# Chunked scan: the decays' exponent is bounded by a minimum on VectorE, the causal mask moves to the scores, and the product with the scores runs one group later

## Chip, cores and metric

One of the eight cores of a Trainium2 chip runs the whole kernel in one launch. The metric is the device time of that core in microseconds, the median of several runs. The other cores are idle.

## Reference, cut to what matters

The reference computes two transformer-like layers over 512 tokens of width 1024. The change touches one part of the first layer, the state-space scan with 16 heads and 2 groups:

```python
a_cs = jnp.cumsum(a_dt, axis=-1)                                   # a_dt = dt * a, never positive
seg = a_cs[..., :, None] - a_cs[..., None, :]
decay = jnp.exp(jnp.where(causal, seg, -jnp.inf))
scores = jnp.einsum('bclgn,bcsgn->bgcls', cc, bc)
attn = scores[:, :, None] * decay
y_diag = jnp.einsum('bgrcls,bcsgrp->bclgrp', attn, x_dt)
```

For each head, the scores of its group are multiplied by exp(sum at l minus sum at s) where s is not after l, and by zero elsewhere. The sums never grow along the sequence, so the exponent is at most zero wherever the mask lets it through. The kernel uses chunks of 128 tokens, which gives the same y.

## The kernel before

**Work and staging.** TensorE runs one long stream of matmuls. Large products with weights (`gemm`, blocks of 512 columns) are cut into eight slices each. A float32 product is made of three matmuls of rounded parts (high by high, high by low, low by high), so a slice of a feature block holds six matmuls of 512 columns. The smaller steps of the layer (scan, attention, norms) are woven in between the slices. All engines walk through one list of steps, written by a planner (`plan`, line 82, the weave of the scan at line 176), and each engine issues its part of every step in the order of that list and waits on semaphores. An engine's queue is strictly in order, so a wait holds back all that comes behind it on that engine.

**Weights.** SyncE loads a block of weights in two pieces into `wraw` (line 797). ScalarE rounds a piece into `whi` (`round_weights`, line 1278) and VectorE takes the rest, `wlo = wraw - whi` (`rest_of_weights`, line 1632). For block m they are issued at slices 0 and 2 (rounding) and 2 and 4 (rest) of the block before (line 246). SyncE waits for `wlo` before it loads that `wraw` again.

**The scan.** There are four chunks c of 128 tokens and for each of them five steps `("ssd", c, part)`. Steps 0 to 3 each handle a group of four heads, step 4 finishes the chunk. Three slices of the k and q products lie between two steps (four after one of the chunks). The intermediate tiles are one large tensor in SBUF, which the profile calls `arena` (`sc`, `ee`, `xdt`, `xs` and others); PSUM tiles are `bank`. In a step with part below 4:

- TensorE (line 1155): at part 0 two score matmuls. Then the exponents of the group, into one bank of 128 by 512: an identity times a mask tile (0 or -1e30, bfloat16, line 1167), and on top of it a matrix of ones times `b_hi` (line 1170), which gives the running sum at l for four heads. Then, from part 1 on, `y_diag(part - 1)`: four matmuls with `ee` as the stationary operand (line 1146), eight instructions of 64 columns in the profile.
- ScalarE (line 1591): four exponentials from the bank into `ee`, with the negated sum at s as the bias, 128 columns each.
- VectorE: at part 0 a copy of the scores to SBUF (line 2043). Then `ee` times the scores (line 2048), which `y_diag` waits for.
- GpSimd: spreads the sums of a later group into `b_hi` (`decays`, line 2201, operation at line 2207), up to four groups ahead, and at part 0 makes `xdt`, `xdd` and the skip term (lines 2229, 2233, 2236), 1024 columns each.

Two banks are used in turn for scores, exponents and chunk states (`plan_aux`, `free_aux` at line 861), and each next user waits for the reader of the one before.

**Where the weights' rests lie between the steps of the scan.** In the order of VectorE, between `("ssd", c, 0)` and `("ssd", c, 1)` stands one rest in chunks 0, 1 and 2, and two stand there in chunk 3. Between parts 1 and 2 there is none in any chunk. Between parts 2 and 3 there are two in chunk 0 and one in each of the others. Between parts 3 and 4 there is none in chunk 0 and one in the others. In the order of ScalarE the rounding of the piece for the second of two such rests comes behind the exponentials of the step ahead of it, and so does that for the one rest between parts 2 and 3 of chunk 3.

Of the kernel before, what the change touches and what calls it, by code (L numbers as in the profile page):

```python
# [23 lines left out]
ALU = mybir.AluOpType  # L24
ACT = mybir.ActivationFunctionType
# [6 lines left out]
P = 128  # L32
# [342 lines left out]
def plan_aux():  # L375

    ring = Ring(2)
    for s in STEPS:
        if s[0] == "xturn":
            ring.use(s, "S")  # L380
        if s[0] == "ssd_decay":
            ring.use("decay", "V")
        if s[0] == "ssd":
            _, c, part = s
            if part == 0:
                ring.use(("scores", c), "V")
            if part < 4:
                ring.use(("decay", c, part), "S")
            if part == 4:
                for g in range(2):  # L390
                    if c > 0:
                        ring.use(("y_off", c, g), "V")
                for g in range(2):
                    if c < NT - 1:
                        ring.use(("state", c, g), "V")
    return ring


AUX = plan_aux()
# [106 lines left out]
def emit(nc, dram, spill, out):  # L506
    ctx = ExitStack()
    with ctx:
# [3 lines left out]
        def sem(name):  # L512
            return ctx.enter_context(nc.semaphore(name))
# [9 lines left out]
        b_hi, b_lo = sb("b_hi", [P, NK, T], F32R), sb("b_lo", [P, NK, T], F32R)  # L523
# [27 lines left out]
        bank = [ctx.enter_context(nc.psum_tensor(f"bank{i}", [P, 512], F32)) for i in range(8)]  # L551

        ident = cst[:, CST.at("ident")]
        tri = cst[:, CST.at("tri")]
# [6 lines left out]
        identb = cstb[:, CSTB.at("ident")]  # L561
        strict = cstb[:, CSTB.at("strict")]
        after = cstb[:, CSTB.at("after")]
# [13 lines left out]
        sc = mem(60, [2, P])  # L577
        ee = mem(61, [2, 4, P])
# [85 lines left out]
        acs_n = small(64)  # L664
# [19 lines left out]
        s_sw = sem("s_small_weights")  # L684
        s_cst, s_ident = sem("s_constants"), sem("s_identity")
        s_tri, s_hg = sem("s_decays_spread"), sem("s_hgrn_gated")
        s_x = [sem(f"s_x{t}") for t in range(NT)]
        s_row = {name: sem("s_row_" + name) for name in ROWS}
        s_yz, s_spill, s_back = sem("s_gated"), sem("s_residual_stored"), sem("s_residual_back")
# [160 lines left out]
        def _(pe):  # L850
            def mm(o, lhsT, rhs, start, stop, **kw):
                return nc.tensor.matmul(o, lhsT, rhs, start=start, stop=stop, **kw)  # L852
# [290 lines left out]
            def ssd(c, part):  # L1143
                ts = slice(P * c, P * c + P)

                def y_diag(j):
                    pe.wait_ge(s_attn, 4 * c + j + 1)
                    if j == 0:
                        pe.wait_ge(s_xd, 2 * c + 1)
                        if c >= 1:  # L1150
                            pe.wait_ge(s_y, c)
                    for i in range(4):
                        h = 4 * j + i
                        last = mm(bank[6 + j // 2][:, (h % 8) * HD:(h % 8) * HD + HD], ee[:, j % 2, i, :],
                                  xdt[:, c % 2, h * HD:h * HD + HD], True, True)
                    last.then_inc(s_yd, 1)

                if part == 0:
                    pe.wait_ge(s_cx, XC)
                    ps = free_aux(("scores", c))  # L1160
                    for g in range(2):
                        last = mm(ps[:, P * g:P * g + P], bct[:, g, ts], bct[:, 2 + g, ts], True, True)
                    last.then_inc(s_aux, 1)
                if part < 4:
                    pe.wait_ge(s_cst, 32)
                    ps = free_aux(("decay", c, part))
                    mm(ps[:, :], identb, after.unsqueeze(1).to_broadcast([P, 4, P]), True, False)
                    n = 4 * c + part
                    pe.wait_ge(s_tri, n + 1)
                    mm(ps[:, :], ones_r, b_hi[:, n % 4, :], False, True).then_inc(s_aux, 1)  # L1170
                    if part >= 1:
                        y_diag(part - 1)
                if part == 4:
                    if c > 0:
                        pe.wait_ge(s_st, 2 * c)
                        for g in range(2):
                            ps = free_aux(("y_off", c, g))
                            mm(ps[:, :], bct[:, 2 + g, ts], state[:, g, :], True, True).then_inc(s_aux, 1)
                    y_diag(3)
                    if c < NT - 1:  # L1180
                        pe.wait_ge(s_xd, 2 * c + 2)
                        for g in range(2):
                            ps = free_aux(("state", c, g))
                            mm(ps[:, :], btok[:, c, P * g:P * g + P], xdd[:, 512 * g:512 * g + 512], True, True)\
                                .then_inc(s_aux, 1)
# [75 lines left out]
        def _(act):  # L1261
# [254 lines left out]
            for s in STEPS:  # L1516
# [64 lines left out]
                    A(dtend, t64[2], ACT.Exp).then_inc(s_ex, 1)  # L1581
                if s[0] == "ssd" and s[2] < 4:
                    _, c, j = s
                    key = ("decay", c, j)
                    act.wait_ge(s_aux, AUX.at[key] + 1)
                    n_ = 4 * c + j
                    if n_ >= 2:
                        act.wait_ge(s_yd, n_ - 1)
                    for i in range(4):
                        col = SH * c + 4 * j + i  # L1590
                        last = A(ee[:, j % 2, i, :], bank[4 + AUX.slot(key)][:, P * i:P * i + P], ACT.Exp,
                                 bias=acs_n[:, col:col + 1])
                    last.then_inc(s_auxend["S"], 1)
                if s[0] == "stack":
                    act.wait_ge(*end_sem("q"))
                    for i in range(3):
# [13 lines left out]
        def _(dve):  # L1610
# [4 lines left out]
            def link(ins):  # L1615

                chain[0] += 1
                ins.then_inc(s_vc, 1)
                dve.wait_ge(s_vc, chain[0])
# [419 lines left out]
            def ssd(c, part):  # L2039
                if part == 0:  # L2040
                    key = ("scores", c)
                    dve.wait_ge(s_aux, AUX.at[key] + 1)
                    link(v.tensor_copy(sc, bank[4 + AUX.slot(key)][:, 0:2 * P].rearrange("p (a b) -> p a b", b=P)))
                    dve.sem_inc(s_auxend["V"], 1)
                if part < 4:
                    dve.wait_ge(s_auxend["S"], AUX.ends[AUX.at[("decay", c, part)]][1])
                    e = ee[:, part % 2, :, :]
                    v.tensor_tensor(e, e, sc[:, part // 2, :].unsqueeze(1).to_broadcast([P, 4, P]), ALU.mult).then_inc(s_attn, 1)
                if part == 4:
                    bc = lambda t, g: t[:, SH * c + 8 * g:SH * c + 8 * g + 8].unsqueeze(2).to_broadcast([P, 8, HD])  # L2050
                    if c > 0:
                        for g in range(2):
                            key = ("y_off", c, g)
                            dve.wait_ge(s_aux, AUX.at[key] + 1)
                            link(v.tensor_tensor(h64(ytmp[:, g, :]), h64(bank[4 + AUX.slot(key)][:, :]), bc(ecs, g), ALU.mult))
                            dve.sem_inc(s_auxend["V"], 1)
                    dve.wait_ge(s_yd, 4 * c + 4)
                    dve.wait_ge(s_xd, 2 * c + 2)
                    for g in range(2):
                        y, x = ytmp[:, g, :], xs[:, c, 512 * g:512 * g + 512]  # L2060
                        if c > 0:
                            link(v.tensor_tensor(y, y, bank[6 + g][:, :], ALU.add))
                            ins = v.tensor_tensor(x, x, y, ALU.add)
                        else:
                            ins = v.tensor_tensor(x, bank[6 + g][:, :], x, ALU.add)
                    ins.then_inc(s_y, 1)
                    if c < NT - 1:
                        for g in range(2):
                            key = ("state", c, g)
                            if c > 0:  # L2070
                                link(v.tensor_tensor(h64(state[:, g, :]), h64(state[:, g, :]), bc(edec, g), ALU.mult))
                            dve.wait_ge(s_aux, AUX.at[key] + 1)
                            ps = bank[4 + AUX.slot(key)][:, :]
                            if c > 0:
                                ins = v.tensor_tensor(state[:, g, :], state[:, g, :], ps, ALU.add)
                            else:
                                ins = v.tensor_copy(state[:, g, :], ps)
                            ins.then_inc(s_st, 1)
                            dve.wait_ge(s_st, 2 * c + g + 1)
                            dve.sem_inc(s_auxend["V"], 1)  # L2080
# [253 lines left out]
```

## Time and profile before

| | before |
|---|---|
| median of 3 runs | 1382.84 us (1381.85 to 1383.66) |
| the profiled execution's own time | 1382.09 us |
| span in the profile | 1380.3 us |
| TensorE matmul busy | 1358.2 us (98%) |
| VectorE busy | 756.0 us (55%) |
| ScalarE busy | 609.0 us (44%) |
| GpSimd busy | 57.0 us (4%) |
| the scan's steps | from 97.94 us to about 213 us of the span |

The profiled execution is 0.75 us under the median, and 1.8 us of it lie outside the span. Engines overlap, so busy times do not add up. Starts and durations of matmuls are modelled, and a matmul is shown as longer than the distance to the next one, because they are pipelined: what counts is the distance between starts. "Idle before" at the end of a row names what the engine waited for. The granted clock of TensorE is 1.0 of full speed (2.4 GHz) in all 40 slices of the page.

### The profile page before, as it was taken

To read this page: it belongs to the slowest core of one execution; us is meant where nothing else is said; L and a number is where in the kernel's file an instruction comes from. 1 tells how busy PE (TensorE), PEld (TensorE's weight loads), DVE (VectorE), ACT (ScalarE), POOL (GpSimd) and SP (SyncE) were. 2 spreads that over 40 slices of the span, in tenths; PEclk is the share of its full clock that TensorE was granted. 3 is DMA by queue.
4 is the path that set the end of the run, shared out by engine and by line. 5 is a ranking of instruction groups with operands and counts; after the bars stand their busy time and mean duration, and the time that the engine had idled before them with its cause. 6 is when DMAs were issued, how large, how long until landed. Compare 5 with 4: busy or idle time off the path is not lost. (4 is left out here: it accounts for less than half of the span.)

```text
span 1380.3 us, 17992 instructions
## 1 busy us (share of the span) xinstructions
PE 1358.2 (98%) x7051; PEld 1127.5 (82%) x7055; DVE 756.0 (55%) x1180; ACT 609.0 (44%) x1129; POOL 57.0 (4%) x38
## 2 busy tenths in 40 slices
PE   9999999999999999999999999999999999999999
PEld 7888778888888888887778777888898888888887
DVE  5775554457656563435457776767555334443333
ACT  6554332457777533224426567773243222221221
POOL 0025310000000000000010000000000000000000
PEclk9999999999999999999999999999999999999999
DMA  4222223252111344232441100102313332232323
GB/s 167 91 77 76 63 76 99 84 145 69 47 47 62 110 150 147 92 101 71 149 133 62 61 17 16 32 1 107 123 62 107 96 103 92 92 106 93 101 82 107
DMA packets 35349, 121.27 MB, mean 88 GB/s; under 512 B 3908, under 2 KB 5188, under 8 KB 35010
## 3 DMA queue, kind: packets, MB, share of 16 engines
q1 hardware_dynamic: 34690, 119.07, 26.6%
q10 hardware_dynamic: 576, 1.05, 0.4%
q8 instruction: 57, 0.93, 0.3%
q14 instruction: 26, 0.21, 0.1%
HBM read 112.77 MB, written 4.19 MB: 85 GB/s over the span
## 5 line engine op out<-in xcount | busy, mean ns | idle before, releaser
L852 PE MATMUL bank<-a_hi,whi 128*128 128x512 f32 (+1 forms) x880 | 345.9, 393 | 0.5 <-DVE a_lo L2132 0.5
L852 PE MATMUL bank<-a_hi,wlo 128*128 128x512 f32 (+1 forms) x880 | 336.7, 383 | 0.0
L852 PE MATMUL bank<-a_lo,whi 128*128 128x512 f32 (+1 forms) x880 | 336.1, 382 | 0.0
L1278 ACT ACTIVATE whi<-wraw 128x1024 fp32r<-128x1024 f32 x194 | 196.8, 1044 | 191.8 <-PE bank L852 162.2
L1632 DVE TENSOR_TENSOR wlo<-wraw,whi 128x1024 fp32r<-128x1024 f32 x194 | 241.2, 1253 | 66.5 <-ACT whi L1278 61.4
L852 PE MATMUL bank<-arena 128*128 128x128 f32 (+5 forms) x1332 | 184.3, 284 | 8.1 <-DVE arena L1994 2.6
L852 PEld LDWEIGHTS bank<-a_hi,wlo 128*128 128x128 f32 x880 | 165.4, 188 | 32.5
L852 PEld LDWEIGHTS bank<-a_hi,whi 128*128 128x128 f32 x880 | 165.8, 188 | 31.7 <-issue 2.4
L852 PEld LDWEIGHTS bank<-a_lo,whi 128*128 128x128 f32 x880 | 165.8, 188 | 30.8 <-issue 1.4
L852 PEld LDWEIGHTS bank<-arena 128*128 128x128 f32 (+1 forms) x1332 | 164.7, 189 | 18.0 <-issue 6.4
L852 PE MATMUL bank<-whi,a_hi 128*128 128x512 f32 x288 | 114.7, 398 | 1.6 <-DVE wlo L1632 0.8
L852 PE MATMUL bank<-whi,a_lo 128*128 128x512 f32 x288 | 112.4, 390 | 0.0
L852 PE MATMUL bank<-wlo,a_hi 128*128 128x512 f32 x288 | 112.2, 389 | 0.0
L852 PE MATMUL bank<-whi,b_hi 128*128 128x512 f32 x240 | 93.8, 391 | 0.0
L852 PE MATMUL bank<-whi,b_lo 128*128 128x512 f32 x240 | 93.4, 389 | 0.0
L852 PE MATMUL bank<-wlo,b_hi 128*128 128x512 f32 x240 | 93.4, 389 | 0.0
L2113 DVE TENSOR_TENSOR_SCAN arena<-arena 128x128 f32<-128x128 f32 (+1 forms) x64 | 52.7, 823 | 58.4 <-ACT arena L1414 58.2
L1327 ACT ACTIVATE b_hi<-arena 128x512 fp32r<-128x512 f32 x30 | 19.0, 634 | 130.2 <-DVE arena L1742 118.3
L1296 ACT ACTIVATE arena<-bank 128x512 f32<-128x512 f32 x50 | 29.8, 597 | 80.8 <-PE bank L852 80.7
L852 PEld LDWEIGHTS bank<-whi,a_hi 128*128 128x128 f32 x288 | 54.1, 188 | 13.7 <-issue 1.8
L1732 DVE TENSOR_TENSOR arena<-arena,bank 128x512 f32<-128x512 f32 x32 | 22.0, 687 | 76.2 <-PE bank L852 76.0
L852 PEld LDWEIGHTS bank<-whi,a_lo 128*128 128x128 f32 x288 | 54.0, 188 | 11.6
(257 smaller groups left out, 1748.0 us busy)
## 6 DMA issues: line engine op xcount, KB each, us to landing
wraw<-in_wblk SPq DMA_DIRECT2D x190, 512.0 KB, 3.8
arena<-in_x SPq DMA_DIRECT2D x4, 512.0 KB, 6.1
arena<-in_x SPq DMA_DIRECT2D x1, 2048.0 KB, 7.9
spill<-arena SPq DMA_DIRECT2D x4, 512.0 KB, 7.8
arena<-spill SPq DMA_DIRECT2D x1, 2048.0 KB, 9.4
out<-arena SPq DMA_DIRECT2D x8, 256.0 KB, 2.5
arena<-arena SPq DMA_DIRECT2D x2, 896.0 KB
arena<-in_w1k SPq DMA_DIRECT2D x1, 1024.0 KB, 7.2
```

Source lines behind the costliest of these rows:

```text
L852: return nc.tensor.matmul(o, lhsT, rhs, start=start, stop=stop, **kw)
L1278: A(whi[n % 2][:, cols], wraw[i][:, 0:cols.stop - cols.start], ACT.Copy).then_inc(s_hi, 1)
L1296: ins = A(sgt[:, k % 2, :], bank[BANK[g]][:, :], ACT.Sigmoid, bias=bias)
L1327: A(b_hi[:, c, :], tt[:, p % 2, :], ACT.Copy).then_inc(s_tround, 1)
L1632: v.tensor_tensor(wlo[n % 2][:, cols], wraw[i][:, 0:cols.stop - cols.start], f32(whi[n % 2][:, cols]), ALU.subtract).then_inc(s_lo, 1)
L1732: v.tensor_tensor(x, x, ps[:, :], ALU.add).then_inc(s_end["V"], 1)
L2113: v.tensor_tensor_scan(w[:, ::-1], fail[:, ::-1], sig[:, ::-1], 0.0, ALU.mult, ALU.add)\
```

## The change

The mask product on TensorE is gone. Its place is taken by a minimum on VectorE, from the bank into `ee`, of the sum at l and the sum at the row's own s (`t64[0]`, which holds it for every row), so that the later exponential is at most one where the mask would be. The scores are multiplied by the causal matrix `tri` where they were copied. The exponentials work in place on `ee` in SBUF. The product with the scores for group part - 1 is issued on VectorE at the start of step part, ahead of the minimum of the group of that step, and for the last group at the start of step 4. The bank of the exponents is now released by VectorE. Two semaphores are new.

```diff
--- before.py
+++ after.py
@@ -385,7 +385,7 @@
             if part == 0:
                 ring.use(("scores", c), "V")
             if part < 4:
-                ring.use(("decay", c, part), "S")
+                ring.use(("decay", c, part), "V")
             if part == 4:
                 for g in range(2):
                     if c > 0:
@@ -684,6 +684,7 @@
         s_sw = sem("s_small_weights")
         s_cst, s_ident = sem("s_constants"), sem("s_identity")
         s_tri, s_hg = sem("s_decays_spread"), sem("s_hgrn_gated")
+        s_clamp, s_dexp = sem("s_exponents_clamped"), sem("s_decays_made")
         s_x = [sem(f"s_x{t}") for t in range(NT)]
         s_row = {name: sem("s_row_" + name) for name in ROWS}
         s_yz, s_spill, s_back = sem("s_gated"), sem("s_residual_stored"), sem("s_residual_back")
@@ -1162,12 +1163,10 @@
                         last = mm(ps[:, P * g:P * g + P], bct[:, g, ts], bct[:, 2 + g, ts], True, True)
                     last.then_inc(s_aux, 1)
                 if part < 4:
-                    pe.wait_ge(s_cst, 32)
                     ps = free_aux(("decay", c, part))
-                    mm(ps[:, :], identb, after.unsqueeze(1).to_broadcast([P, 4, P]), True, False)
                     n = 4 * c + part
                     pe.wait_ge(s_tri, n + 1)
-                    mm(ps[:, :], ones_r, b_hi[:, n % 4, :], False, True).then_inc(s_aux, 1)
+                    mm(ps[:, :], ones_r, b_hi[:, n % 4, :], True, True).then_inc(s_aux, 1)
                     if part >= 1:
                         y_diag(part - 1)
                 if part == 4:
@@ -1581,16 +1580,11 @@
                     A(dtend, t64[2], ACT.Exp).then_inc(s_ex, 1)
                 if s[0] == "ssd" and s[2] < 4:
                     _, c, j = s
-                    key = ("decay", c, j)
-                    act.wait_ge(s_aux, AUX.at[key] + 1)
-                    n_ = 4 * c + j
-                    if n_ >= 2:
-                        act.wait_ge(s_yd, n_ - 1)
+                    act.wait_ge(s_clamp, 4 * c + j + 1)
                     for i in range(4):
                         col = SH * c + 4 * j + i
-                        last = A(ee[:, j % 2, i, :], bank[4 + AUX.slot(key)][:, P * i:P * i + P], ACT.Exp,
-                                 bias=acs_n[:, col:col + 1])
-                    last.then_inc(s_auxend["S"], 1)
+                        last = A(ee[:, j % 2, i, :], ee[:, j % 2, i, :], ACT.Exp, bias=acs_n[:, col:col + 1])
+                    last.then_inc(s_dexp, 1)
                 if s[0] == "stack":
                     act.wait_ge(*end_sem("q"))
                     for i in range(3):
@@ -2040,12 +2034,23 @@
                 if part == 0:
                     key = ("scores", c)
                     dve.wait_ge(s_aux, AUX.at[key] + 1)
-                    link(v.tensor_copy(sc, bank[4 + AUX.slot(key)][:, 0:2 * P].rearrange("p (a b) -> p a b", b=P)))
+                    link(v.tensor_tensor(sc, bank[4 + AUX.slot(key)][:, 0:2 * P].rearrange("p (a b) -> p a b", b=P),
+                                         tri.unsqueeze(1).to_broadcast([P, 2, P]), ALU.mult))
                     dve.sem_inc(s_auxend["V"], 1)
+                if part >= 1:
+                    j = part - 1
+                    dve.wait_ge(s_dexp, 4 * c + part)
+                    e = ee[:, j % 2, :, :]
+                    v.tensor_tensor(e, e, sc[:, j // 2, :].unsqueeze(1).to_broadcast([P, 4, P]), ALU.mult).then_inc(s_attn, 1)
                 if part < 4:
-                    dve.wait_ge(s_auxend["S"], AUX.ends[AUX.at[("decay", c, part)]][1])
-                    e = ee[:, part % 2, :, :]
-                    v.tensor_tensor(e, e, sc[:, part // 2, :].unsqueeze(1).to_broadcast([P, 4, P]), ALU.mult).then_inc(s_attn, 1)
+                    key, n = ("decay", c, part), 4 * c + part
+                    dve.wait_ge(s_aux, AUX.at[key] + 1)
+                    if n >= 2:
+                        dve.wait_ge(s_yd, n - 1)
+                    link(v.tensor_tensor(ee[:, part % 2, :, :], bank[4 + AUX.slot(key)][:, :].rearrange("p (a b) -> p a b", b=P),
+                                         t64[0][:, 4 * n:4 * n + 4].unsqueeze(2).to_broadcast([P, 4, P]), ALU.min))
+                    dve.sem_inc(s_auxend["V"], 1)
+                    dve.sem_inc(s_clamp, 1)
                 if part == 4:
                     bc = lambda t, g: t[:, SH * c + 8 * g:SH * c + 8 * g + 8].unsqueeze(2).to_broadcast([P, 8, HD])
                     if c > 0:
```

## Rows read from the trace of the kernel before

**Rows 1.** Windows of the scan: sum and number of instructions of each engine, PE clock.

```profile
97.00:213.00 116.00, 116.00 (x561) 92.18 (x560) 62.98 (x65) 43.19 (x96) 43.59 (x25) 1.00 0.23 73
```

**Rows 2.** Timeline of TensorE around two groups of chunk 0: start us, duration us.

```profile
102.69 0.39 PE L852 MATMUL bank<-a_hi,wlo 128*128 128x512 f32 x1
...
102.92 0.39 PE L852 MATMUL bank<-cstb 128*128 128x512 bf16 x1
...
103.38 1.00 PE L852 MATMUL bank<-arena 128*128 128x64 f32 x8
...
108.40 0.39 PE L852 MATMUL bank<-cstb 128*128 128x512 bf16 x1
```

**Rows 3.** Groups of VectorE: the page, and by form from 98 to 212 us.

```profile
L1632 DVE TENSOR_TENSOR wlo<-wraw,whi 128x1024 fp32r<-128x1024 f32 x194 | 241.2, 1253 | 66.5 <-ACT whi L1278 61.4
...
L2055 DVE TENSOR_TENSOR arena<-bank,stat 128x512 f32<-128x512 f32 x6 | 4.2, 692 | 9.1 <-PE bank L852 9.1
```

**Rows 4.** Timeline of chunk 0's first group without TensorE; last, the skip term of chunk 3.

```profile
97.94 2.15 DVE L1632 TENSOR_TENSOR wlo<-wraw,whi 128x1024 fp32r<-128x1024 f32 x1 [1.23 <-ACT whi L1278]
...
98.95 2.89 POOL L2233 TENSOR_TENSOR arena<-arena,stat 128x1024 f32<-128x1024 f32 x1
...
99.35 1.28 ACT L1591 ACT_TABLE_LOAD   x1
...
100.00 0.41 DVE L2043 COPY arena<-bank 128x256 f32<-128x256 f32 x1
...
100.65 1.14 ACT L1591 ACTIVATE arena<-bank,stat 128x128 f32<-128x128 f32 x4
...
101.82 0.69 DVE L2048 TENSOR_TENSOR arena<-arena 128x512 f32<-128x512 f32 x1 [1.41 <-ACT arena L1591]
...
101.92 2.35 POOL L2236 TENSOR_TENSOR arena<-arena,vec 128x1024 f32<-128x1024 f32 x1
...
102.43 2.92 DVE L1632 TENSOR_TENSOR wlo<-wraw,whi 128x1024 fp32r<-128x1024 f32 x1
...
104.23 2.02 POOL L2207 TENSOR_TENSOR b_hi<-b_hi,cst 128x512 fp32r<-128x512 f32 x1
...
187.28 1.90 POOL L2236 TENSOR_TENSOR arena<-arena,vec 128x1024 f32<-128x1024 f32 x1 [18.69 <-DVE arena L2075]
```

**Rows 5.** Timeline of another stage: TensorE waits for VectorE and restarts.

```profile
942.45 0.68 DVE L1994 COPY arena<-bank 128x512 f32<-128x512 f32 x1
...
943.19 2.50 PE L852 MATMUL bank<-arena 128*128 128x128 f32 x20 [0.85 <-DVE arena L1994]
```

**Rows 6.** Timeline of chunk 1's first group.

```profile
125.19 2.76 POOL L2236 TENSOR_TENSOR arena<-arena,vec 128x1024 f32<-128x1024 f32 x1
...
126.75 0.43 DVE L2043 COPY arena<-bank 128x256 f32<-128x256 f32 x1 [0.56 <-PE bank L852]
...
127.91 1.04 POOL L2207 TENSOR_TENSOR b_hi<-b_hi,cst 128x512 fp32r<-128x512 f32 x1
...
131.55 1.00 PE L852 MATMUL bank<-arena 128*128 128x64 f32 x8
```

**Rows 7.** Timeline of chunk 2's first group.

```profile
158.05 2.77 POOL L2236 TENSOR_TENSOR arena<-arena,vec 128x1024 f32<-128x1024 f32 x1
...
158.97 0.41 DVE L2043 COPY arena<-bank 128x256 f32<-128x256 f32 x1
...
162.76 1.00 PE L852 MATMUL bank<-arena 128*128 128x64 f32 x8
```

**Rows 8.** Timeline of chunk 3's first group.

```profile
187.82 0.43 DVE L2043 COPY arena<-bank 128x256 f32<-128x256 f32 x1 [0.62 <-PE bank L852]
...
189.14 1.04 POOL L2207 TENSOR_TENSOR b_hi<-b_hi,cst 128x512 fp32r<-128x512 f32 x1
...
189.28 1.08 ACT L1278 ACTIVATE whi<-wraw 128x1024 fp32r<-128x1024 f32 x1
...
192.62 1.00 PE L852 MATMUL bank<-arena 128*128 128x64 f32 x8
```

## The prediction

> **What bounds the kernel now.** I read the page first, then the windows of the scan, then TensorE's timeline there, and last the timelines of the other engines around each product with the scores. The windows show TensorE busy for 116.00 us of 116.00, at full clock, with VectorE at 62.98 and ScalarE at 43.19 [rows 1]. So a matmul taken out of this stretch is worth its pitch at once, and any wait put on TensorE costs its length. TensorE's timeline gives the pitch as the distance between starts: 102.69 to 102.92 is 0.23 us for one matmul of 512 columns, and from the mask product at 102.92 to `y_diag` at 103.38 there are two such pitches, 0.46 us [rows 2]. The question is whether VectorE, which gets more to do and in another order, still delivers each `ee` before TensorE asks for it.
>
> **What it removes.** Sixteen mask products on TensorE at 0.23 us are 3.7 us, all on the path that sets the end. The wait for the constants that goes with them had long been met. Nothing is issued to a DMA queue by what moves, and SyncE's and GpSimd's own lists stay as they are.
>
> **What it adds.** Sixteen minimums from a bank with a broadcast operand from SBUF. The nearest row is of that very kind, bank and statistics to `arena`, 128 by 512: 692 ns [rows 3], in all 11 us on VectorE. The four score copies become products from the bank, at the same size, and I take the copy's 0.41 us [rows 4]. VectorE would be busy for 74 of the 116 us, so its load alone is covered. The exponentials stay at about 1.14 us for four [rows 4], now from SBUF; up to 0.2 us more would not change the sum, since below something else than they comes last in three chunks of four. Every bank is given back after the minimum, which is sooner than after the exponentials.
>
> **How VectorE and GpSimd share.** This sets the price of the new order. Alone, a `wlo` takes about 1.25 us on average [rows 3]. The one at 102.43 took 2.92 us and ended at 105.35, which is 1.08 after GpSimd's skip term ended at 104.27 (101.92 + 2.35). That skip term in turn took 2.35 where the same one of chunk 3, with no such product beside it, took 1.90, as it began to work only when VectorE's product ended at 102.51 [rows 4]. So in these rows each waits for the whole instruction of the other, then takes its turn, and VectorE's next one in line comes behind GpSimd's waiting one. The Trainium skill's page "SBUF — State Buffer", section "Who interferes with whom", says the same: a VectorE instruction with two SBUF inputs and a GpSimd one that reads SBUF lock each other out for whole instructions; the trace agrees with that. The score copy ran 0.41 us while GpSimd held the port [rows 4], so I take it that an instruction with a bank as source is not held.
>
> **The moved product.** The new order on VectorE is minimum, then the rests of weights that stand between the steps, then the product, then the next minimum. Before, the product came ahead of the rests. Where GpSimd is working, just after part 0 of each chunk, this is a row of turns. I work out when `y_diag(0)` can start, against when TensorE reaches it; the latter is 0.46 us earlier than now, as two mask products lie before it. A restart is put at 0.1 us after VectorE's end, since a wait elsewhere ended at 943.19 behind a copy that ended at 943.13 [rows 5].
> - Chunk 0. `wlo` ends at 100.09, scores at 100.41, minimum from 100.45 to 101.14. The next `wlo` waits for GpSimd's `xdd` to end at 101.84, and ends 1.08 later at 102.92. The skip term holds the port until 104.69 (1.77, as from 102.51 to 104.27). The product then takes 0.55 and ends at 105.24. The exponentials are done by 102.4 (by 103.7, if the table load of 1.28 us waited for them, which decides nothing). TensorE is there at 102.92, and restarts at 105.34: **2.4 us** lost [rows 4, 2].
> - Chunk 1. Scores end at 127.18, minimum at 127.94. GpSimd's spread begins at 127.91 and holds until 128.95; `wlo` to 130.03; the next spread about 1.0 to 131.0; product to 131.6. TensorE is there at 131.09: **0.6 us** [rows 6].
> - Chunk 2. Scores end at 159.38, minimum at 160.1. The skip term holds until 160.82; `wlo` to 161.9; a spread to 162.9; product to 163.4. TensorE is there at 162.30: **1.2 us** [rows 7].
> - Chunk 3. Scores end at 188.25, minimum at 189.0, exponentials at 190.2. The rounding behind them takes 1.08 to 191.3, which the second `wlo` needs. The first `wlo` runs from 189.18 to 190.3; two spreads in turn until 192.2, as the second `wlo` is not ready when the port comes free at 191.2; `wlo` to 193.3; product to 193.85. TensorE is there at 192.16: **1.8 us** [rows 4, 8].
>
> Between the later parts there is time enough. From one group's matmul to the next it was 5.48 us (102.92 to 108.40) [rows 2] and will be 5.25, and `y_diag` comes 0.23 behind: 5.5. The longest chain is chunk 0 from part 2 to 3 and the like in chunk 3: matmul 0.4, minimum 0.7, exponentials 1.15, rounding 1.08, `wlo` 1.25, product 0.6, together 5.2. It just fits, with 0.3 us to spare; I put 0 to 0.6 us on both together. All others lack the rounding, and fit with 2 us to spare even if GpSimd takes a turn.
>
> **Sum.** Less 3.7, plus 2.4 + 0.6 + 1.2 + 1.8 = 6.0: 2.3 us longer. Against the profiled execution's 1382.1 that is 1384.4; it stood 0.75 below the median, so against 1382.8 it is **1385.1 us**, 0.17% more. A measurement of this kernel can tell about 0.2% from no change, 2.8 us, so this is at the upper edge of "same". Nothing later gives the lost time back: it is matmuls that start later.
>
> **What isn't in the trace.** A minimum or product with one operand in a bank and one in SBUF while GpSimd works. From below it costs 0.69 or 0.41 us as taken above. From above it is held as the `ee` product was. The skill's page (same section) has the rule that one SBUF input at most does not contend; by it the sum stays as worked out, by the other it is that of the first rival. I take the lower end, because of the score copy, and keep the upper for the range.
>
> **Rivals.**
> - *The minimum and the masked scores are held by GpSimd too.* For: the second operand comes from SBUF, as that of the held ones did. Against: the copies ran free, but they have no second operand. Then, with the same turns, the product of chunk 0 ends at 106.8 instead of 105.2, chunk 1 at 132.2, chunk 2 (the skip term is under way when the scores come) at about 166.3, chunk 3 at about 195.1. The stalls are 4.0, 1.2, 4.1 and 3.0, together 12.3, less 3.7: 1391.4 us, slower. It turns slower as soon as the stalls pass 6.5 us. Slower by over 0.2% comes also from the forecast's own case if the small unknowns (restarts, semaphores that two more instructions pass on, the two tight chains) all cost: 0.6 us more is enough.
> - *The product is on time.* VectorE gets the port ahead of GpSimd when both wait, so that the rest and the product run back to back; then chunk 0 costs 0.7, chunk 3 about 0.9 for the rounding, the others nothing: 1382.8 − 3.7 + 1.6 = 1380.7. With no stall at all it is 1379.1. For: 1.4 to 2.4 us of idle time stand ahead of the products now. Against: the row at 102.43, in which the waiting GpSimd came first.
> - *TensorE's freed time is lost elsewhere, with no stall at `y_diag`:* the next waits would have to grow. TensorE had no wait in the stretch [rows 1], so I give this little.
>
> **How the numbers follow.** My case 0.65, spread from 1383.4 to 1388 (restart, tight chains, who is first in chunk 1). Held minimums 0.12, product on time 0.20, the last 0.03. Of my case about half lies above 1385.6. So slower by over 0.2%: 0.32 + 0.10 = 0.42. Faster by over 0.2% (under 1380.1): most of the product-on-time case with few stalls, 0.12. Same: 0.46. The range runs from 1379.5, which takes in nearly all of the on-time case, to 1389.5, which takes in my case's upper end and the weaker half of the held ones. The likeliest case's own range is 1383.4 to 1388.
>
> **What would show it.** Right: TensorE idle four times, just ahead of `y_diag(0)` of each chunk, released by the product on VectorE, longest in chunk 0; the period between groups at 5.25 us; a minimum of 0.69 us while GpSimd works; products of part 0 behind a `wlo`. Wrong: no idle time there and the scan 3.7 us shorter; a minimum of over 1 us; or idle time ahead of another part's `y_diag`, the two tight chains first.

## The result and the profile after

| | before | changed kernel |
|---|---|---|
| median | 1382.53 us (8 runs, 1381.59 to 1383.96) | 1386.79 us (8 runs, 1385.24 to 1389.31) |
| ratio to before | | 1.0031 [1.0022, 1.0040] |
| profiled execution, its span | 1382.09, 1380.3 us | 1385.24, 1383.4 us |
| VectorE busy | 756.0 us | 766.9 us |
| mean granted clock of the profiled execution | 1.000 | 0.997 |

The changed kernel is slower by 0.31%, 4.3 us. That is above the 0.2% line, and inside the range. The forecast was 1385.1, just under the line. The profiled execution is the fastest of the eight. Of all executions below one, in experiment 3, took 6525 us at a mean granted clock of 0.197; its profile is undisturbed up to 267 us, it counts in the median there (1384.32 us, 1384.2 without it) and not in the ratio.

TensorE had no wait in the scan before. In the changed kernel this is the whole list of its waits there (waiting line, what released it: us in total, times, longest):

```profile
PE bank L853 <- DVE arena L2044: 5.0, 4, 2.2
```

L2044 is the product of `ee` with the scores. TensorE's timeline of the changed kernel has the four waits, each ahead of the `y_diag(0)` of a chunk, with the idle time in brackets:

```profile
104.76 1.10 PE L853 MATMUL bank<-arena 128*128 128x64 f32 x8 [2.20 <-DVE arena L2044]
...
134.26 0.99 PE L853 MATMUL bank<-arena 128*128 128x64 f32 x7 [0.28 <-DVE arena L2044]
...
165.76 1.10 PE L853 MATMUL bank<-arena 128*128 128x64 f32 x8 [0.92 <-DVE arena L2044]
...
196.55 1.10 PE L853 MATMUL bank<-arena 128*128 128x64 f32 x8 [1.57 <-DVE arena L2044]
```

How the first of them comes about is in the timeline of the other engines in chunk 0 of the changed kernel, which answers to [rows 4]:

```profile
98.43 2.89 POOL L2238 TENSOR_TENSOR arena<-arena,stat 128x1024 f32<-128x1024 f32 x1
...
99.48 0.41 DVE L2037 TENSOR_TENSOR arena<-bank,cst 128x256 f32<-128x256 f32 x1
...
100.03 0.69 DVE L2050 TENSOR_TENSOR arena<-bank,stat 128x512 f32<-128x512 f32 x1
...
100.91 1.28 ACT L1586 ACTIVATE arena<-arena,stat 128x128 f32<-128x128 f32 x4 [0.80 <-DVEq L2053]
100.96 1.44 DVE L1626 TENSOR_TENSOR wlo<-wraw,whi 128x1024 fp32r<-128x1024 f32 x1 [0.24 <-DVE arena L2050]
...
101.40 2.76 POOL L2241 TENSOR_TENSOR arena<-arena,vec 128x1024 f32<-128x1024 f32 x1
...
102.17 0.39 PE L853 MATMUL bank<-b_hi 128*128 128x512 f32 x1
102.32 2.38 DVE L2044 TENSOR_TENSOR arena<-arena 128x512 f32<-128x512 f32 x1
104.12 4.93 POOL L2212 TENSOR_TENSOR b_hi<-b_hi,cst 128x512 fp32r<-128x512 f32 x4
```

The masked scores (L2037) and the minimum (L2050) take 0.41 and 0.69 us in the midst of GpSimd's `xdd` (98.43 to 101.32). The exponentials are done at 102.19. The rest of the weights ends at 102.40, and the product behind it takes 2.38 us, of which it works only the last 0.54: GpSimd's skip term has its turn until 104.16. TensorE, which issued its last matmul at 102.17, restarts at 104.76.

A second thing shows in the windows of the changed kernel (busy us with instructions of TensorE, weight loads, VectorE, ScalarE, GpSimd; then the granted clock):

```profile
106.00:108.00 2.00, 2.00 (x7) 1.56 (x6) 1.19 (x1) 0.78 (x3) 2.00 (x3) 0.59 0.00 0
108.00:110.00 2.00, 2.00 (x7) 1.59 (x6) 0.15 (x1) 1.55 (x2) 2.00 (x2) 0.56 0.00 0
110.00:196.00 86.00, 83.78 (x398) 66.43 (x396) 55.01 (x61) 30.77 (x66) 30.17 (x18) 1.00 0.20 64
196.00:200.00 4.00, 3.45 (x16) 2.99 (x17) 1.79 (x3) 1.28 (x4) 0.00 (x0) 0.81 0.65 207
200.00:215.00 15.00, 15.00 (x68) 11.94 (x68) 5.21 (x7) 5.66 (x12) 0.00 (x0) 0.94 0.20 72
```

TensorE's clock was 1.00 in the whole scan before [rows 1]. Now it falls from 2.4 GHz to the level of 1.2 GHz twice, shortly behind the waits of 2.20 and 1.57 us; behind those of 0.28 and 0.92 us it stays up. In the timeline the distance between starts goes from 0.23 to 0.43 us:

```profile
106.53 0.63 PE L853 MATMUL bank<-a_hi,whi 128*128 128x512 f32 x1
...
106.96 0.63 PE L853 MATMUL bank<-a_lo,whi 128*128 128x512 f32 x1
...
107.39 0.63 PE L853 MATMUL bank<-a_hi,wlo 128*128 128x512 f32 x1
```

The windows give the price of a fall: 2 × 0.41 + 2 × 0.44 = 1.7 us for the first, 4 × 0.19 + 15 × 0.06 = 1.7 us for the second.

**The sum, measured.** From the first score matmul to the start of the last addition of `y` the scan took 115.53 us before (97.94 to 213.47) and takes 121.32 us now (97.41 to 218.73), 5.8 more. From matmul to matmul, the waits cost 2.36, 0.44, 1.08 and 1.73 us, together 5.6. With −3.7 for the mask products and 3.4 for the clock that is 5.3. The 0.5 us left are found in two places. Behind a wait `y_diag` itself takes 0.91 us to the next matmul (104.76 to 105.67), and 0.81 where it doesn't wait (103.38 to 104.19 before), which is 0.1 in each of four chunks. And a mask product was worth 0.22 us rather than 0.23, 3.5 us in all (see below).

The profiled span grew by only 3.1 us, because this execution was 0.5 us ahead when the scan began, took 1.8 us less in a stage between about 650 and 710 us, and made up 0.4 us in smaller amounts behind it. In that stage ScalarE's roundings wait for weights to land, here the same one in the kernel before and in the changed kernel:

```profile
656.08 1.06 ACT L1278 ACTIVATE whi<-wraw 128x1024 fp32r<-128x1024 f32 x1 [3.24 <-DMA wraw<-in_wblk]
660.99 1.06 ACT L1277 ACTIVATE whi<-wraw 128x1024 fp32r<-128x1024 f32 x1 [2.90 <-DMA wraw<-in_wblk]
```

So what the stage takes differs with the landings. From a wait of TensorE at 651 us to one at 787 us (times of the kernel before) it is 135.9 us before, 134.1 in the changed kernel and 136.5 in another execution of the changed kernel (below), whose time is 1387.8. The saving isn't there each time, and a difference of 2 us between the spans of two profiles is no measure of a change to the scan.

### The profile page after: what moved, and what is told of

Same layout as the page of the kernel before. It is cut to its first block and busy times, and to the rows that moved or that the text cites. A ratio compares the mean times of both kernels' runs of the same rounds, so it can differ in the third digit from the quotient of the medians.

```text
span 1383.4 us, 18008 instructions
## 1 busy us (share of the span) xinstructions
PE 1358.5 (98%) x7035; PEld 1128.3 (82%) x7039; DVE 766.9 (55%) x1196; ACT 611.5 (44%) x1129; POOL 56.9 (4%) x38
## 2 busy tenths in 40 slices
DMA packets 35349, 121.27 MB, mean 88 GB/s; under 512 B 3908, under 2 KB 5188, under 8 KB 35010
```

## The experiments

Experiments 1 to 4 ran on one chip, where the kernel before had 1382.25 us (27 runs). The second profile of experiment 3 and experiment 5 are from another, where it had 1382.85 us (15 runs). A ratio with its interval is not the quotient of the two medians given, and can differ from it by 0.0008, about 1 us.

The scan, from the first score matmul to the start of the last addition of `y`, can be measured in each profile without the rest of the kernel. "Sum" is −3.5 us for the mask products where they are gone, plus the waits from matmul to matmul, 0.1 for each wait and 1.7 for each fall of the clock:

| profile | waits, us | falls in the scan | sum, us | scan against before's 115.53, us |
|---|---|---|---|---|
| changed kernel | 5.6 (4) | 2 | 5.9 | 5.8 |
| changed kernel, run again | 5.6 (4) | 2 | 5.9 | 5.7 |
| experiment 1 | 2.6 (2) | 0 | −0.7 | −0.6 |
| experiment 2 | 3.7 (3) | 0 | 4.0 | 4.0 |
| experiment 3, second profile | 4.6 (4) | 0 | 1.5 | 1.5 |
| experiment 4 | 2.0 (3) | 0 | −1.2 | −1.1 |
| experiment 5 | 5.6 (4), most of it filled | 0 | 2.5 | 2.6 |

These few terms account for the scan of every kernel within 0.2 us. The prices of the terms come from the same profiles, but one set of them fits all seven.

### 1. The product put back, ahead of the rests

The changed kernel, with the product in its old place:

```diff
-                if part >= 1:
-                    j = part - 1
-                    dve.wait_ge(s_dexp, 4 * c + part)
-                    e = ee[:, j % 2, :, :]
-                    v.tensor_tensor(e, e, sc[:, j // 2, :].unsqueeze(1).to_broadcast([P, 4, P]), ALU.mult).then_inc(s_attn, 1)
...
                     dve.sem_inc(s_clamp, 1)
+                    dve.wait_ge(s_dexp, n + 1)
+                    e = ee[:, part % 2, :, :]
+                    v.tensor_tensor(e, e, sc[:, part // 2, :].unsqueeze(1).to_broadcast([P, 4, P]), ALU.mult).then_inc(s_attn, 1)
```

> The changed kernel, with VectorE's product with the scores put back into its own step, right behind the wait for the exponentials and ahead of the rests of weights; the minimum, the masked scores and the exponentials in place stay. Theory 1 (the product's place behind the rests, with GpSimd in between, makes the waits): the wait ahead of y_diag(0) falls to about 1.5 us in chunk 0 (GpSimd's skip term begins while VectorE waits for the exponentials), 0.1 in chunk 1, 0.6 in chunk 2 and 0 in chunk 3, the granted clock stays at 1.00 or falls once at most, and the time is 1380.5 to 1382.5 us against 1382.5 before. Theory 2 (the longer chain matmul, minimum, exponentials, product makes them, in whatever order): waits of over 1 us stay in three or four chunks and the time is 1385 us or more.

Measured: 1381.24 us (11 runs), ratio 0.9997 [0.9988, 1.0006], no different from before. Against the changed kernel's 1.0031 that is 0.34%, 4.7 us. The mean clock is 1.000 in nine of the runs and 0.999 and 0.997 in the others. Two waits are left, in chunks 0 and 2, the second 0.3 us longer than expected:

```profile
104.29 0.88 PE L853 MATMUL bank<-arena 128*128 128x64 f32 x6 [1.35 <-DVE arena L2051]
...
163.26 0.99 PE L853 MATMUL bank<-arena 128*128 128x64 f32 x7 [0.94 <-DVE arena L2051]
```

The place of the product is the cause of the loss. But the minimum has a price of its own even here. It puts a link into the chain from the exponents to the product, and at part 0 the product then meets GpSimd's skip term:

```profile
101.29 1.28 ACT L1586 ACTIVATE arena<-arena,stat 128x128 f32<-128x128 f32 x4 [0.80 <-DVEq L2048]
101.78 1.91 POOL L2239 TENSOR_TENSOR arena<-arena,vec 128x1024 f32<-128x1024 f32 x1
...
102.61 1.63 DVE L2051 TENSOR_TENSOR arena<-arena 128x512 f32<-128x512 f32 x1 [1.50 <-ACT arena L1586]
```

Before, the product ran in 0.69 us at 101.82, ahead of the skip term [rows 4]; here it is 0.8 us later and takes 1.63, to 104.24.

### 2. The kernel before with nothing but the move

```diff
-                if part < 4:
-                    dve.wait_ge(s_auxend["S"], AUX.ends[AUX.at[("decay", c, part)]][1])
-                    e = ee[:, part % 2, :, :]
-                    v.tensor_tensor(e, e, sc[:, part // 2, :].unsqueeze(1).to_broadcast([P, 4, P]), ALU.mult).then_inc(s_attn, 1)
+                if part >= 1:
+                    j = part - 1
+                    dve.wait_ge(s_auxend["S"], AUX.ends[AUX.at[("decay", c, j)]][1])
+                    e = ee[:, j % 2, :, :]
+                    v.tensor_tensor(e, e, sc[:, j // 2, :].unsqueeze(1).to_broadcast([P, 4, P]), ALU.mult).then_inc(s_attn, 1)
```

> The kernel before, with mask product, score copy and exponentials from the bank as they were, and only VectorE's product with the scores moved one group later. Theory 1: by the same turns with GpSimd TensorE waits ahead of y_diag(0) about 2.0 us in chunk 0, 0 in chunk 1, 0.7 in chunk 2, 1.3 in chunk 3, 4.0 us together, and where a wait is long the granted clock falls to half for a while, 1.7 us each time: 1386.5 to 1389 us. Theory 2 (the minimum's chain is to blame): no waits over 0.5 us, 1382.5 us as before.

Measured: 1388.26 us (5 runs), ratio 1.0044 [1.0031, 1.0056], 6.0 us slower than before on the same chip. The order alone costs at least about as much as the whole change, whose ratio was 1.0031 and, run again, 1.0039; the intervals overlap, so that more than this isn't shown. The minimum isn't needed for the loss. The waits:

```profile
105.26 1.10 PE L852 MATMUL bank<-arena 128*128 128x64 f32 x8 [1.75 <-DVE arena L2049]
...
165.37 1.10 PE L852 MATMUL bank<-arena 128*128 128x64 f32 x8 [0.47 <-DVE arena L2049]
...
196.46 1.10 PE L852 MATMUL bank<-arena 128*128 128x64 f32 x8 [0.97 <-DVE arena L2049]
```

Each is 0.2 to 0.3 us less than expected. The profiled execution, 1386.80 us and the fastest of the five, kept the full clock in spite of its wait of 1.75 us; the other four have mean clocks of 0.998 and 0.999 and are 1 to 2.4 us longer.

### 3. GpSimd's `xdd` and skip term one step later

The changed kernel; GpSimd makes the two in the step of part 1, behind the first product:

```diff
+                if s[0] == "ssd" and s[2] == 1:
+                    c = s[1]
+                    bc = lambda t: t[:, SH * c:SH * c + SH].unsqueeze(2).to_broadcast([P, SH, HD])
+                    pool.wait_ge(s_attn, 4 * c + 1)
...
```

> The changed kernel, with VectorE's order as it is there, but GpSimd's xdd and skip term moved from step 0 to step 1 of each chunk, behind a wait for the first product. Theory 1, and that GpSimd's turns are what makes the rest and the product late: the waits ahead of y_diag(0) fall to 0.1 us in chunk 0, 0 in chunks 1 and 2, and about 1.0 in chunk 3, where the rounding behind the exponentials holds the rest; granted clock 1.00; 1379.5 to 1381 us. If the order alone makes them, without GpSimd, over 4 us of waits stay and the time is 1385 us or more.

Measured: 1384.32 us (11 runs), ratio 1.0015 [1.0006, 1.0024]. Better than the changed kernel, but well above what was expected, and the clock of 1.00 that I had expected is there in only six of the ten runs behind the ratio; the other four show 0.997 or 0.999. A second profile, on the other chip, was to show where the time went:

> The kernel with GpSimd's two operations moved to step 1, for a profile of a whole undisturbed execution. By the first profile's scan, the waits are 0.4 us in chunk 0 and 1.2 us in chunk 3, none in chunks 1 and 2 ahead of y_diag(0), but 2.0 us ahead of y_diag(2) of chunk 0 and 0.4 us in chunk 1 behind the moved operations; 1383 to 1385 us.

It took 1383.65 us (one run, at full clock) and has four waits, the same ones as the first:

```profile
103.66 1.10 PE L853 MATMUL bank<-arena 128*128 128x64 f32 x8 [0.41 <-DVE arena L2044]
...
116.44 1.10 PE L853 MATMUL bank<-arena 128*128 128x64 f32 x8 [2.01 <-DVE arena L2044]
...
144.34 0.88 PE L853 MATMUL bank<-arena 128*128 128x64 f32 x6 [0.37 <-DVE arena L2044]
...
194.51 1.10 PE L853 MATMUL bank<-arena 128*128 128x64 f32 x8 [1.16 <-DVE arena L2044]
```

At `y_diag(0)` the waits fell as expected: 0.41 in chunk 0, none in 1 and 2, 1.16 in chunk 3, where two rests and a rounding stand ahead of the product. So GpSimd's turns are the second part of the mechanism. What was missed is the wait of 2.01 us at `y_diag(2)` of chunk 0. There two rests stand ahead of the product. The moved operations run from 103.68 to 107.57 us and push back what stands behind them in GpSimd's queue, spreads (L2212) and the `xdt` of the next chunk (L2234). That `xdt` began at 109.01 in the changed kernel, with the rests of this place (112.85 and 115.06, 1.23 us each) free of it; now it begins 1.96 us later and meets them:

```profile
110.97 2.89 POOL L2234 TENSOR_TENSOR arena<-arena,stat 128x1024 f32<-128x1024 f32 x1
112.36 2.57 DVE L1626 TENSOR_TENSOR wlo<-wraw,whi 128x1024 fp32r<-128x1024 f32 x1 [0.27 <-ACT whi L1277]
...
113.82 2.02 POOL L2212 TENSOR_TENSOR b_hi<-b_hi,cst 128x512 fp32r<-128x512 f32 x1
114.86 1.52 DVE L2044 TENSOR_TENSOR arena<-arena 128x512 f32<-128x512 f32 x1
```

### 4. Both: the product ahead of the rests, GpSimd's work one step later

The edits of experiments 1 and 3 together.

> The product back in its own step and GpSimd's two operations moved to step 1, with the minimum in place of TensorE's mask. Theory 1: no wait ahead of any y_diag, the whole of 16 matmuls of 0.23 us is gained: 1378.9 us, against 1382.5 before. Theory 2: waits remain, 1382 us or more.

Measured: 1381.24 us (11 runs, 1379.16 to 1381.72), ratio 0.9985 [0.9976, 0.9994]. This is the one version whose ratio to the kernel before lies below 1 with its whole interval, by 0.15% (0.07% by the medians), which is less than the 0.2% that I called distinguishable. Against experiment 1 its median is the same, its ratio 0.0012 lower with an interval that overlaps, and its scan 0.5 us shorter in the profile, so a small gain from moving GpSimd's work besides is likely and not shown. It falls 2.3 us short of the 1378.9 that I had expected. Three waits are left: 0.41 us in chunk 0, 0.54 at `y_diag(3)` of chunk 0 and 0.60 in chunk 3. The second comes from two rests that are held in turns for 4.91 us, again by the next chunk's `xdt` (L2232) and a spread:

```profile
112.07 2.35 POOL L2232 TENSOR_TENSOR arena<-arena,stat 128x1024 f32<-128x1024 f32 x1
112.58 4.91 DVE L1626 TENSOR_TENSOR wlo<-wraw,whi 128x1024 fp32r<-128x1024 f32 x2
114.38 2.02 POOL L2210 TENSOR_TENSOR b_hi<-b_hi,cst 128x512 fp32r<-128x512 f32 x1
```

### 5. TensorE kept busy while it waits

The question left by the result was whether the idle time brings the clock down. The changed kernel issues 8, 1, 3 and 6 matmuls that nobody reads, into a free bank, ahead of its wait in chunks 0 to 3:

```diff
+                        for _ in range((8, 1, 3, 6)[c]):
+                            mm(bank[6][:, :], ones_r, ones_r.unsqueeze(1).to_broadcast([P, 4, P]), True, True)
```

> The changed kernel, with TensorE kept at work while it would wait for the product: 8, 1, 3 and 6 matmuls of 512 columns, whose results nobody reads, ahead of the wait of y_diag(0) in chunks 0 to 3, at 0.23 us each, a little less than the waits of 2.36, 0.44, 1.08 and 1.73 us by starts. They lengthen nothing if they lie within the waits. If the falls of the granted clock follow from the idle time, it stays at 1.00 through the scan, the waits shrink to under 0.6 us each, and the time falls by 1.7 us for each fall that is missing: 1384 to 1385.5 us, with the unfilled kernel at 1386.8. If the falls have another cause, they stay, and the time is that of the unfilled kernel.

Beside it, on the same chip, the changed kernel as it is:

> The changed kernel itself once more, on the same chip and beside the same runs as the filled one. Expected 4 to 4.5 us above the kernel before, at least one stretch at half the granted clock in nearly every execution, and the four waits ahead of y_diag(0) as in its first profile: 2.2, 0.3, 0.9 and 1.6 us.

Measured: 1384.54 us (11 runs), ratio 1.0014 [1.0005, 1.0023], against 1387.77 us (5 runs), ratio 1.0039 [1.0026, 1.0051], which is 4.9 us above the kernel before by the medians, a little more than expected. The clock is 1.000 in all 11 runs of the filled kernel and 0.997 or 0.998 in all 5 of the other. With the windows of the filled kernel first,

```profile
106.00:110.00 4.00, 4.00 (x23) 3.41 (x23) 1.63 (x2) 2.83 (x6) 4.00 (x4) 1.00 0.10 39
198.00:202.00 4.00, 4.00 (x24) 3.39 (x22) 1.19 (x2) 0.60 (x1) 0.00 (x0) 1.00 0.15 57
```

and those of the changed kernel, run again, second:

```profile
106.00:110.00 4.00, 4.00 (x14) 3.25 (x14) 1.34 (x1) 1.91 (x6) 4.00 (x4) 0.61 0.01 4
198.00:202.00 4.00, 4.00 (x12) 3.10 (x12) 0.69 (x1) 0.83 (x3) 0.00 (x0) 0.59 0.28 107
```

the filler takes away nothing but the idle time, since each `y_diag(0)` still starts only when its product is there: waits of 0.40, 0.24 and 0.21 us remain behind the filler in chunks 0, 2 and 3. It gives back 3.2 us, which are the two falls at 1.7 us; the scan alone is 3.2 us shorter too (118.10 against 121.27). The waits of the changed kernel run again are 2.20, 0.26, 0.92 and 1.57 us, nearly the same as in the first profile.

## Why the prediction was right, and where it fell short

**The result's sign and mechanism.** The mechanism is the one of the likeliest case: the product stands behind the rests of weights, and both take turns with GpSimd. Experiments 1 and 3 take away one half of it each, and the waits at `y_diag(0)` shrink or go, each within 0.4 us of what I expected.

**The mask products.** Their gain is real, 3.5 us of the 3.7. From one group's matmul to the next it was 5.48 us [rows 2] and is now 5.26, 0.22 less, where neither a wait nor a fall of the clock lies between:

```profile
139.38 0.40 PE L853 MATMUL bank<-b_hi 128*128 128x512 f32 x1
...
144.64 0.40 PE L853 MATMUL bank<-b_hi 128*128 128x512 f32 x1
```

Experiment 1, whose scan has this gain and 2.8 us of waits with what follows them, is 0.6 us shorter in the scan, and 1.0 us (by the medians) or 0.4 us (by the ratio) in the whole.

**The four waits.** Forecast 2.4, 0.6, 1.2, 1.8, together 6.0; measured from matmul to matmul 2.4, 0.4, 1.1, 1.7, together 5.6. In chunk 0 the turns came in the order that I had worked out from the row of 2.92 us [rows 4]. The scan began 0.53 us earlier than before; with that added, the product ended at 105.23 (forecast 105.24) and TensorE restarted at 105.29 (105.34).

**What GpSimd holds.** The minimum took 0.69 us and the masked scores 0.41 beside a working GpSimd; over the scan the 16 minimums take 677 to 694 ns:

```profile
L2050 DVE TENSOR_TENSOR arena<-bank,stat x16: 677/692/694, 100.0 to 208.9; 128x512 f32<-128x512 f32 x16
L2044 DVE TENSOR_TENSOR arena<-arena x16: 679/693/2382, 102.3 to 211.1; 128x512 f32<-128x512 f32 x16
```

(Smallest, median and largest in ns.) The products, with both operands in SBUF, go up to 2382. So the first rival fell on its own ground, and the rule that one SBUF input at most does not contend (the Trainium skill, "SBUF — State Buffer", "Who interferes with whom") agrees with these rows.

**The tight chains** cost nothing: no wait stands there in the changed kernel. The distance between groups is the 5.26 us shown above, forecast 5.25. The exponentials from SBUF took 1.28 us for four instead of 1.14, which was allowed for.

**What failed** is the step "Less 3.7, plus 2.4 + 0.6 + 1.2 + 1.8 = 6.0: 2.3 us longer". It prices each wait at its length and has no term for the clock. The granted clock fell behind the two longest waits, and this cost 3.4 us more in the profiled execution, 3.2 us by experiment 5. With 3.4 the sum is 5.7 for the scan, where 5.8 was measured (that they are so close is luck: the waits were 0.4 shorter than forecast, the mask products were worth 0.2 less and `y_diag` takes 0.4 more behind its waits); it is what carries the result over the 0.2% line. Since the range had room for unknown costs, it held, but the likeliest value was 1.7 us short of the median and on the wrong side of the line, and I had given "same" 0.46 and slower 0.42. The sentence "Nothing later gives the lost time back" holds for no wait that I found, yet the stage in which the weights' landings decide took 1.8 us less than before in one profile of the changed kernel and 0.6 more in the other, and the 4.3 us of the medians are less than the scan's 5.8. Whether later stages give some of it back on average is open. The other half of the question, whether something behind a wait takes more, was not asked.

**My expectation of experiment 3** failed because I followed the moved GpSimd work at the place it left, and not what it pushes back behind the place it came to.

**The second rival** (product on time) fell: in chunk 0 the waiting GpSimd instruction again came ahead of VectorE's next one. **The third** (no stall at `y_diag`) fell with the list of waits, in which there is nothing else.

**Open.** Length alone doesn't say which wait brings the clock down. Behind 1.75 us in experiment 2 and behind 2.01 us at 116.44 in experiment 3 it stayed up in the profiled executions, behind 1.57 us it fell in two of two; and the eight runs of the changed kernel have mean clocks from 0.996 to 0.999, so that the loss isn't the same each time. A fall need not come from the scan either. At about 787 us of the kernel before, TensorE waits 1.52 us for ScalarE, and every profile that is undisturbed there has this wait. In seven of these eight the clock stays up behind it; in that of experiment 4 it falls (windows as above):

```profile
785.29 0.69 PE L1028 MATMUL bank<-cst,arena 128*128 128x128 f32 x2 [1.52 <-ACT arena L1500]
784.00:788.00 4.00, 2.71 (x8) 2.23 (x9) 3.63 (x10) 2.90 (x13) 0.00 (x0) 0.66 0.19 38
788.00:790.00 2.00, 2.00 (x16) 1.86 (x15) 0.15 (x2) 0.00 (x0) 0.00 (x0) 0.83 0.54 186
```

That is 4 × 0.34 + 2 × 0.17 = 1.7 us again. It may be what five of the 27 runs of the kernel before have, which show 0.998 though that kernel has no wait in the scan; none of them was profiled, so this isn't shown. For the same reason a mean clock below 1.000 in a run without a profile doesn't tell that the scan brought it down.

## What to carry to other kernels

Work taken from the engine at the limit is a gain only if its producers keep pace with the earlier time at which it now asks: here 3.5 us of matmuls went, and VectorE's product, put behind fill-in work, came late four times, 5.6 us in all. Put the instruction that the busy engine waits for ahead of fill-in work on its queue, and when work is moved on an engine that shares a port, follow it to the place where it lands and see what it pushes back behind it. Price a wait of one to two microseconds on TensorE at its length plus a possible fall of the clock behind it, in this kernel 1.7 us each.

## What I had not expected of the hardware

- A wait of 1.57 us on a TensorE that was busy otherwise was followed by a stretch at the 1.2 GHz level that cost 1.7 us, about as much again as the wait. Unread matmuls in the wait keep the clock up, and pay: 1384.54 against 1387.77 us.
- Between the end of the minimum and VectorE's next instruction pass about 0.2 us, as in `[0.24 <-DVE arena L2050]` above; the sum had counted 0.03 to 0.1 us there. In this place VectorE waits for the minimum's own end and then raises two semaphores; which of the two takes the time wasn't separated.
